# Second recurrent branch: the half-row key-value products of one chunk pair placed between the chunk matrices, the later ones in groups of eight among the output products

## The reference

```python
CHUNK = 64
...
    intra = jnp.where(causal, jnp.einsum('bhnid,bhnjd->bhnij', q_in, k_in), 0.0)
    last = cum[..., -1:, :]
    k_dec = k * jnp.exp(last - cum)[..., None]
...
    def step(state, xs):
        qi, ki, vi, ai, di = xs
        o = jnp.einsum('bhcd,bhde->bhce', qi, state) + jnp.einsum('bhij,bhje->bhie', ai, vi)
        state = di[..., :, None] * state + jnp.einsum('bhcd,bhce->bhde', ki, vi)
        return state, o
```

## Time and profile before

| | |
|---|---|
| median of three runs | 2386.37 us |
| the profiled execution | 2387.17 us, of which the span from first to last instruction is 2384.9 us |
| busy in the span: TensorE, VectorE, ScalarE | 95%, 63%, 53% |
| mean granted TensorE clock in the span | 0.98 |
| this branch, from the first transposed key to the next product | 1378.49 to 1429.94 us |
| of this, chunk matrices | 1382.04 to about 1389.35 us |
| of this, the loop over t | 1390.23 to about 1429 us |

### The profile page before, as it was taken

The page is one execution under the profiler, slowest core; times in us unless marked ns, Lnnn a source line. Parts: engine busy times, 40 slices in busy tenths (PEclk is TensorE's granted clock), DMA queues, the critical chain, the costliest instruction groups (busy, mean ns, idle before and its releaser), DMA issues. The chain is left out here.

```text
span 2384.9 us, 29398 instructions
## 1 busy us (share of the span) xinstructions
PE 2264.3 (95%) x11234; PEld 1794.4 (75%) x11234; DVE 1501.0 (63%) x1863; ACT 1269.3 (53%) x1680; POOL 279.8 (12%) x273
## 2 busy tenths in 40 slices
PE   7999899999998999999999999999995999999994
PEld 6878558777777768998888878888774777777773
DVE  4435742559986677656334545355337899988886
ACT  4334532478873445652324423235324888888884
POOL 2000000023320212340000000000001211122210
PEclk9999999999999999999999999999996999999997
DMA  7122103422324332001322312334125999999995
GB/s 238 64 71 89 44 10 97 131 88 89 99 70 168 125 124 110 16 2 38 104 88 89 105 36 72 123 123 159 68 86 209 379 407 408 408 402 400 400 403 188
DMA packets 119817, 377.40 MB, mean 158 GB/s; under 512 B 9609, under 2 KB 38593, under 8 KB 94497
## 3 DMA queue, kind: packets, MB, share of 16 engines
q1 hardware_dynamic: 106432, 332.49, 37.7%
q0 software_dynamic: 12768, 37.13, 4.6%
q10 hardware_dynamic: 512, 6.34, 0.7%
HBM read 363.02 MB, written 21.02 MB: 161 GB/s over the span
## 5 line engine op out<-in xcount | busy, mean ns | idle before, releaser
L2243 DVE TENSOR_TENSOR w_lo<-raw,w_hi 128x2048 fp32r<-128x2048 f32 x118 | 270.3, 2290 | 459.9 <-ACT w_hi L1595 459.6
L1595 ACT ACTIVATE w_hi<-raw 128x2048 fp32r<-128x2048 f32 x118 | 225.8, 1914 | 413.4 <-PE bank L850 367.4
L850 PE MATMUL bank<-hT_hi,w_hi 128*128 128x512 f32 x512 | 201.1, 393 | 4.6 <-DVE hT_lo L2307 2.3
L850 PE MATMUL bank<-hT_lo,w_hi 128*128 128x512 f32 x512 | 200.3, 391 | 0.0
L850 PE MATMUL bank<-hT_hi,w_lo 128*128 128x512 f32 x512 | 200.2, 391 | 0.0
L1059 PE MATMUL bank<-hT_hi,w_hi 128*128 128x512 f32 x448 | 180.3, 402 | 1.3 <-DVE hT_lo L2307 1.3
L1059 PE MATMUL bank<-hT_hi,w_lo 128*128 128x512 f32 x448 | 174.5, 390 | 0.0
L1059 PE MATMUL bank<-hT_lo,w_hi 128*128 128x512 f32 x448 | 174.5, 390 | 0.0
L3032 DVE TENSOR_TENSOR e_lo<-eraw,e_hi 128x2048 fp32r<-128x2048 f32 x62 | 141.9, 2290 | 36.4 <-ACT e_hi L2123 34.7
L2916 DVE TENSOR_TENSOR e_lo<-raw,e_hi 128x2048 fp32r<-128x2048 f32 x64 | 146.6, 2291 | 8.2 <-ACT e_hi L2106 7.9
L2916 DVE TENSOR_TENSOR w_lo<-raw,w_hi 128x2048 fp32r<-128x2048 f32 x64 | 144.2, 2287 | 8.9 <-ACT w_hi L2106 8.8
(11 more groups left out here) (572 smaller groups left out, 5322.4 us busy)
## 6 DMA issues: line engine op xcount, KB each, us to landing
raw<-expert_w_gate SPq DMA_DIRECT2D x64, 1024.0 KB, 11.3
raw<-expert_w_up SPq DMA_DIRECT2D x64, 1024.0 KB
eraw<-expert_w_down SPq DMA_DIRECT2D x64, 1024.0 KB
raw<-w_in SPq DMA_DIRECT2D x40, 1024.0 KB, 5.1
raw<-even_w_in SPq DMA_DIRECT2D x18, 1024.0 KB, 5.2
raw<-odd_w_in SPq DMA_DIRECT2D x16, 1024.0 KB, 5.4
raw<-even_w_out SPq DMA_DIRECT2D x8, 1024.0 KB, 5.0
raw<-odd_w_out SPq DMA_DIRECT2D x8, 1024.0 KB, 5.4
```

Of the source, the lines that this page charges most:

```text
L850: mm = pe.matmul(out, st, mv, start=first and x == 0, stop=last and x == 2)
L1595: act.activation(w_hi[m % SPL][:], raw[n % RAW][:], ACT.Copy).then_inc(sem("hi_done"), 1)
L2243: dve.tensor_tensor(w_lo[m % SPL][:], raw[split_of[m] % RAW][:], f32(w_hi[m % SPL][:]), ALU.subtract).then_inc(sem("lo_done"), 1)
```

## The change

The products of a tile are now made by a function, `chunk_products(t, part)`, with four parts of four heads: part 0 and 1 are s = 0, part 2 and 3 are s = 1, and part p goes into bank p as before. For tile 0 the parts follow the chunk matrices of heads 4, 5, 6 and 7, each once the mask of head `part` has read the bank (a new event `h_mask`, counted by the masks of VectorE). TensorE no longer waits at the barrier but for all eight masks. The parts of tile t + 1 are made two by two: parts 0 and 1 behind the output of head 5 of tile t, parts 2 and 3 behind the output of head 7. The number of products and outputs is unchanged.

```diff
@@ events that share a semaphore
-        "y_part": ("y_mix", KD + 4 + NQ),
+        "h_mask": ("y_mix", KD + 4 + NQ),
+        "y_part": ("y_mix", KD + 4 + NQ + HEADS),
@@ TensorE
+        def chunk_products(t, part):
+
+            s, hg = part // 2, part % 2
+            if t:
+                pe.wait_ge(*after("hs_S", HEADS * (2 * (t - 1) + s) + 4 * hg + 4))
+            else:
+                pe.wait_ge(*after("h_mask", part + 1))
+                pe.wait_ge(*after("h_kdev", 4 * hg + 4))
+            r = slice(s * QC, s * QC + QC)
+            for h in range(4 * hg, 4 * hg + 4):
+                mm = pe.matmul(psum[part][:, (h % 4) * P:(h % 4) * P + P], hkd[r, h, t], hv[r, t, h * P:h * P + P],
+                               start=True, stop=True)
+            mm.then_inc(sem("hs_kv"), 1)
+
         for h in range(HEADS):
             pe.wait_ge(*after("h_kdev", h + 1))
...
             mm.then_inc(sem("h_in"), 1)
-        stage()
+            if h >= 4:
+                chunk_products(0, h - 4)
+        stage(wait=False)
+        pe.wait_ge(*after("h_mask", HEADS))
         for t in range(NT):
-            for s in range(2):
-                for h in range(HEADS):
-                    if h % 4 == 0 and t:
-                        pe.wait_ge(*after("hs_S", HEADS * (2 * (t - 1) + s) + 4 * (h // 4) + 4))
-                    r = slice(s * QC, s * QC + QC)
-                    mm = pe.matmul(psum[2 * s + h // 4][:, (h % 4) * P:(h % 4) * P + P], hkd[r, h, t], hv[r, t, h * P:h * P + P],
-                                   start=True, stop=True)
-                    if h % 4 == 3:
-                        mm.then_inc(sem("hs_kv"), 1)
             for h in range(HEADS):
...
                 if h % 4 == 3:
                     mm.then_inc(sem("hs_ope"), 1)
+                if t + 1 < NT and h in (5, 7):
+                    chunk_products(t + 1, h - 5)
+                    chunk_products(t + 1, h - 4)
         stage()
@@ VectorE
             dve.tensor_tensor(hintra[:, :, h], psum[h][:].rearrange("p (t j) -> p t j", j=P),
-                              m_hgrn.unsqueeze(1).to_broadcast([P, NT, P]), ALU.mult)
+                              m_hgrn.unsqueeze(1).to_broadcast([P, NT, P]), ALU.mult).then_inc(sem("h_mask"), 1)
```

## The result

The changed kernel takes 2418.47 us (median of 20 runs, 2386.33 to 2422.55), the kernel before 2385.44 us (median of 20 runs, 2383.29 to 2417.94). The ratio is 1.0111 with a 95% interval from 1.0088 to 1.0134; the medians differ by 33.0 us or 1.4%. Both kernels have two groups of times with nothing between them: 18 of the 20 runs of the changed kernel lie above 2410 us and 2 near 2387, of the kernel before 2 of 20 lie above 2410 us. (A ratio weighs every run and not the middle one, except those over 1.5% above the fastest of their kernel, so that the two groups of times can set it apart from the quotient of the medians.) The forecast was 2387.6 us, 2383.7 to 2391.1: the change made the kernel slower by far more than that.

The account below looks back on a forecast made before the run. TensorE, busy 95% of the span, was taken as the bound, with only a 0.88 us barrier gap to win. Part 1 (+0.97) and part 2 (+0.27) added 1.24 to 2386.37, giving 2387.6 us, range 2383.7 to 2391.1.

Parts of the forecast that it names:

- the long fall as a rival of 0.04: Gap at the barrier brings a long clock fall into the loop; 10 us at half clock, 2392.6 us; chance 0.04.
- a clock in the branch below 1.00: Sign named in advance that the forecast would be wrong: granted clock below 1.00 in the branch; no size given.
- 0.22 for a short one: Clock falls once behind the new 1.7 us gap, about 4 us at 0.58; +2.9 us, 2389.3; chance 0.22.
- The gap, +0.97 us for part 1: At the barrier, first tile's products between chunk matrices delay the first output by 0.97 us, bounds +0.75 to +1.09.
- The loop, +0.27 us for part 2: In the loop, products in eights add three switches from products to outputs at 0.09 us each; bounds 0 and 0.27.
- the cover of parts 2 and 3: Between heads 7 and 0, 1.75 us of products hide VectorE's 0.95 us step; without it up to 2.9 us.
- The unit of 0.104 us: Start-to-start spacing of product instructions in a loop turn, from 32 instructions taking 3.50 us.
- The rival of the open weight loads (0.05): Six more switches from half-row products to full-row work each leave a 0.19 us load open; +2.0 us, 2388.3; chance 0.05.
- my sum of 1.24: Whole kernel: +0.97 for part 1 and +0.27 for part 2 make +1.24 us, bounds +0.5 and +1.4.
- The shift carried to the end: Behind the loop TensorE is busy throughout, so a shift of the loop's end reaches the kernel's end whole.

Follow-up runs that it names:

- the run with the dense matmuls: The changed kernel with 16 dense fp32r matmuls of 512 columns added behind the outputs of tile 0; 2401.59 us, ratio 1.0066.
- the one execution of 8024.93 us: Tenth run of the changed kernel with six more fp32 products filling TensorE's gap before the last mask's wait; median of those 10 runs 2390.8 us.

## Why the prediction was wrong, step by step

**The step that failed: the long fall as a rival of 0.04.** The mechanism stood there with its price formula, 0.5 us for each us at half clock: 72 us at half gives 36 as a bound, and 28.2 were paid. What was wrong is its chance and its length, 10 us. It was set aside because "the loop is dense, and at 1628 the clock is back at 1.00". A busy share of 100% at full clock says nothing on whether the same work lifts a clock that has fallen. What ran at 1628 were dense fp32r products of 256 columns, and the loop has none; the run with the dense matmuls shows the difference. I took the length of a fall from other stages, 3.4 us at 1624 and 10 us as a guess for a long one, and not from the stage it would fall into. Even there I left out the longest in the trace of the kernel before, which is also one with little work on TensorE:

```profile
1800.00:1840.00 40.00, 14.49 (x76) 12.93 (x76) 28.92 (x67) 11.54 (x12) 3.17 (x2) 0.53 0.70 259
```

The sign that I had named, a clock in the branch below 1.00, is the one that came.

**The chance of a fall.** I had 0.22 for a short one, from three gaps elsewhere of 1.37, 1.95 and 1.79 us, of which only the last fell. These don't order by width, which should have told me that the neighbourhood counts; the right question was how far the gap of this place, 0.88 us and harmless in the profile, was from harm. The table says: 0.16 us for about half of the runs, 0.29 us for all. The runs of before up to then (three, 2384 to 2388) could not show that the kernel already fell in about one run of ten.

**The gap, +0.97 us for part 1.** That the barrier's gap would not be filled but grow was right: 1.45 us for the 1.7 forecast. VectorE's chain from the last mask to the first output is 1394.10 - 1392.29 = 1.81 us for 1.87. But the last mask starts 1391.60 - 1380.41 = 11.19 us behind the first matrix instead of 1389.39 - 1382.04 = 7.35, so +3.84 and not +2.65: a matrix with a part takes 1388.23 - 1386.06 = 2.17 us against 0.89 for a matrix alone, so that putting the part in costs 1.28 where I counted 0.88. The first output is 13.69 - 11.59 = 2.1 us later, not 0.97.

**The loop, +0.27 us for part 2.** At full clock a turn has 10.26 us for 9.72: three times 0.54 is 1.6. Waits for VectorE did not appear, the cover of parts 2 and 3 held.

**The unit of 0.104 us** is behind both. It was a mean over 32 instructions with one change of half in their middle. The rows of the shorter runs show it: 8 take 1.16, so (1.16 - 0.27) / 7 = 0.127 us apart; 16 take 2.05, so 0.119; 32 with one change take 3.50, so 0.104; 32 with 31 changes take 2.06, so 0.058. The eights keep one half in each group and give up the change, and each group pays its first load anew. From 8 to 16 instructions the steady spacing is (1.78 - 0.89) / 8 = 0.111 us, while each group of 8 between the matrices, of products and of matrices alike, lasts 1387.15 - 1386.06 = 1.09 us to the next group, 0.20 more than 8 x 0.111. So ahead of the last mask there are six switches of 0.20 us, in and out, where I had counted three of 0.05: 24 x 0.111 + 6 x 0.20 = 3.86, measured 3.84. The rival of the open weight loads (0.05) had the right sign, +2.0, and about the right price of a switch (0.19) but too few of them, and is nearer to the 3.7 us at full clock than my sum of 1.24. I had dismissed it with a row that showed overlap on one half, which is real but slower than that between halves. The Trainium skill, TensorE: Matmul & The Clock Gate, section Part 3: Packing small matmuls, has loads overlapping only where row groups differ. The trace agrees that different halves overlap far better (0.058 against 0.112 to 0.127 us) and doesn't bear out that on the same half they don't overlap at all: loads of 0.188 us go by at that pace.

**The shift carried to the end** held: +31.9 us in the branch, +33.0 in the median. In the runs that did not fall the change of the median lies within 1 us of that of the branch. Single executions scatter more, and with their clock: in the 65 executions of the kernel before that did not fall and have their clock on record, the mean time goes from 2383.3 us at a mean clock of 0.983 to 2387.8 us at 0.980.

What stays open: why this loop does not bring the clock back when the dense transposes at 766 us do; whether at an equal gap the mixed order makes a fall likelier than the plain one (5 of 12 at 1.04 us and 12 of 12 at 1.17 came from different orders), and the one execution of 8024.93 us.

## What to carry to other kernels

Ahead of a stage of small matmuls, a gap on TensorE has to be priced with the whole stage, not with the gap: 0.3 us more of waiting cost 29 us here, and some matmuls whose result nobody needs were a cure. Ask of such a stage two things: does it hold the clock, and would it bring it back. And products that use half of the rows should alternate between the halves; a mean spacing taken over a run that contains a change of half can't be used for an order without it.

## What the runs showed of the hardware

At half clock the loop's outputs start 1.35 us apart and not 0.79, busy all the time, and the clock did not rise in 65 us of them; sixteen matmuls of 512 columns raised it within 5 us. Elsewhere 24 dense fp32 matmuls of 128 columns on all rows saw it rise too, 4.8 us after the first of them started. Whether the clock fell passed from 0 of 10 to 12 of 12 runs between gaps of 0.85 and 1.17 us, with 10 of 93 at 0.88 and 18 of 20 at 1.45. Matmul instructions on alternating halves of the rows start 0.058 us apart, on one half 0.11 us, and each switch between half-row products and full-row matrices adds 0.20 us.
